# Where the two rings of split weights begin in a partition, in a float32r decoder trunk held by TensorE

## The chip, the cores and the metric

The kernel runs on one core of a Trainium2 chip. The metric is the device time of one execution in microseconds. Two timed runs of the kernel before gave 2196.1 and 2196.19 us, median 2196.14 us.

## The reference

The kernel computes a two-layer decoder trunk on 256 tokens of width 2048, all in float32:

```python
def swiglu(h, w_in, w_out):
    g, u = jnp.split(h @ w_in, 2, axis=-1)
    return (jax.nn.silu(g) * u) @ w_out
...
x = x + gla_mixer(rms_norm(x, attn_norm), gla_w_in, w_alpha2, b_alpha, head_gain, gla_w_out)
x = x + swiglu(rms_norm(x, ffn_norm[0]), ffn_w_in[0], ffn_w_out[0])
k_shared, v_shared = shared_kv(x, kv_norm, w_kv, k_norm)
x = x + diff_attention(rms_norm(x, diff_norm), k_shared, v_shared, diff_w_q, ...)
x = x + swiglu(rms_norm(x, ffn_norm[1]), ffn_w_in[1], ffn_w_out[1])
```

Here `gla_mixer` is gated linear attention in chunks of 64 tokens (4 heads), `shared_kv` one projection to normalised keys and values, and `diff_attention` attention with two softmaxes per head (8 heads). Nearly all the arithmetic is in the eight products of 256 tokens with a weight matrix: 2048 rows by 6144 columns (and 16 for the gate), 2048 by 2048, 2048 by 11264 (`w_in` of the FFN, d_ff is 5632), 5632 by 2048, then the same again with 6144 columns of keys, queries and values.

## The kernel before

**Units.** A weight matrix is worked off in blocks of 512 columns, and each block in units of 256 rows (`UNIT_KT` = 2 tiles of 128). A unit is 128 partitions by 2 x 512 float32, 4 KB in a partition. There are 784 units. SyncE's queue loads a unit into `raw`, a ring of four slots (`SLOTS`). ScalarE copies it to `w_hi` rounded to float32r, the high part (L945), and VectorE subtracts that from `raw` and writes the rest as float32r to `w_lo`, the low part (L1311). `w_hi` and `w_lo` are rings of four slots too, each 16 KB in a partition.

**Products.** The tokens are kept transposed and are split in the same way: `xT[:, 0]` is the high part, `xT[:, 1]` the low part, in tiles of 128 rows by 256 tokens. TensorE holds 128 tokens as the stationary operand (128 float32r, 512 bytes in a partition) and streams 512 columns of the weights (2048 bytes in a partition) as the moving operand. One float32 product is three float32r products, high x high, high x low and low x high, so that a unit takes 2 row tiles x 2 token halves x 3 = 12 matmuls of 128x512:

```python
def unit(src, kt, n_kt, p, slot, u):
    pe.wait_ge(lo_done, u + 1)
    for j in range(UNIT_KT):
        for tb in range(TB):
            hi = src[:, 0, kt + j, tb * P:(tb + 1) * P]
            lo = src[:, 1, kt + j, tb * P:(tb + 1) * P]
            nc.tensor.matmul(acc[p][tb][:, :], hi, w_hi[:, slot, j, :], ...)   # L639
            nc.tensor.matmul(acc[p][tb][:, :], hi, w_lo[:, slot, j, :], ...)   # L640
            last = nc.tensor.matmul(acc[p][tb][:, :], lo, w_hi[:, slot, j, :], ...)   # L641
    last.then_inc(unit_used, 1)
```

`first_unit` (L651, L656) serves the first block and `last_unit` (L667 to L669) the last unit, with the same twelve matmuls in another order. `src` is one of five stationary arrays of the same shape: `xT` (inputs of the GLA, of both FFNs and of keys and values), `g_oT`, `xT_q`, `d_oT` and `hT` (5632 rows, the hidden activations of an FFN). Every matmul is issued with a load of its stationary operand (LDWEIGHTS, engine PEld in the profile), which runs while the matmul before it streams.

**Other matmuls.** Between units stand a few hundred others. Those with plain float32 operands are shown as two instructions for each matmul: the score and value products of both attentions (L762 to L782, L882 to L900) and the transposes of `x` (L678). Those with float32r operands outside the rings are the gate: L727 multiplies `a_w` (stationary, 96 columns, 384 bytes in a partition, sixteen of them one behind the other) with the 256 tokens of `xT` (moving, always at a multiple of 512 bytes), and L740 multiplies `w_gate` (stationary, 128 columns, multiples of 512) with the 256 tokens of `a_T` (moving, at a multiple of 512).

**Order.** The order of the work is written out by hand per engine, with semaphores: TensorE waits for `lo_done` of the unit, ScalarE for the load and for the unit four back to be used, VectorE for ScalarE. The loads wait for `lo_done` of the unit four back.

**Addresses.** Arrays are laid in a partition one behind the other in the order in which `trunk` names them. A helper fills up to a wanted remainder of 512 bytes:

```python
def place(name, rest, stack=ctx):
    base = -(-nc.sbuf_base // 32) * 32
    gap = (rest - base) % 512
    if gap:
        sb(name, [P, gap // 4], F32, stack)
```

It is called with 0 ahead of `x` and ahead of `g_oT`, `hT` and the pair `xT_q`, `d_oT`. `x` (16 KB), `xT` (32 KB) and `raw` (16 KB) are whole multiples of 512, so that `w_hi` and `w_lo` begin at a multiple of 512 as well.

Of the kernel before, what the change touches and what calls it, by code (L numbers as in the profile page):

```python
# [182 lines left out]
def trunk(nc, x_in, attn_norm, gla_w_in, w_alpha2, b_alpha, gla_head_norm, gla_w_out, kv_norm, w_kv, k_norm,  # L183
          diff_norm, diff_w_q, q_norm, lq1, lk1, lq2, lk2, diff_head_norm, diff_w_out, ffn_norm, ffn_w_in,
          ffn_w_out, const_in, out):
    with ExitStack() as ctx:
        def sb(name, shape, dt=F32, stack=ctx):
            return stack.enter_context(nc.sbuf_tensor(name, shape, dt))
# [4 lines left out]
# [6 lines that stand above are left out]
# [3 lines left out]
        x = sb("x", [P, TB, D])  # L202
        xT = sb("xT", [P, 2, KT, S], F32R)
        raw = sb("raw", [P, SLOTS, UNIT_KT, CB])
        w_hi = sb("w_hi", [P, SLOTS, UNIT_KT, CB], F32R)
        w_lo = sb("w_lo", [P, SLOTS, UNIT_KT, CB], F32R)
        tok = sb("tok", [P, TB, CB])
        scratch = sb("scratch", [P, TB * CB])
        junk = sb("junk", [P, CB])
# [1541 lines left out]
```

## Time and profile before

| what | value |
|---|---|
| median of 2 timed runs | 2196.14 us (2196.1 to 2196.19) |
| profiled execution, first to last instruction (span) | 2193.8 us |
| granted TensorE clock, mean over the span | 1.000 |
| PE busy, share of the span, matmul instructions | 2188.1 us, 100%, 9720 |
| weight loads (PEld) busy | 1808.9 us, 82% |
| VectorE, ScalarE, GpSimd busy | 57%, 48%, 13% |
| bytes moved by DMA, mean rate | 447.01 MB, 204 GB/s |

A timed run is 2.3 us longer than the span of the profiled execution, the part that lies around the first and the last instruction. The matmul rows have a modelled end: a matmul of 512 columns is drawn with some 389 ns although the next begins 227 ns after it, so that a busy PE says only that the engine had work. The pace is read from the distance of the starts.

### The profile page before, as it was taken

The numbers are of one execution on the slowest core, as the hardware profiler recorded it, in microseconds if no ns is written. First come the engines' busy times: TensorE is split into PE (matmuls) and PEld (weight loads), VectorE is DVE, ScalarE is ACT, GpSimd is POOL, SyncE is SP. The second block draws the span as 40 slices with busy tenths as digits, with TensorE's granted clock in tenths as the row PEclk, the third lists the DMA queues.
The fourth block names the chain that finished last, engine by engine and source line by source line (L and its number), as shares of the span: only waits on it lengthen the run. The fifth ranks groups of instructions, "written<-read, shape, count | busy, mean of one in ns | idle before, by whom it ended". The sixth has DMA issues, their size and how long they took to land.

```text
span 2193.8 us, 27239 instructions
## 1 busy us (share of the span) xinstructions
PE 2188.1 (100%) x9720; PEld 1808.9 (82%) x9720; DVE 1242.7 (57%) x1460; ACT 1058.2 (48%) x1428; POOL 283.0 (13%) x563
## 2 busy tenths in 40 slices
PE   9999999999999999999999999999999999999999
PEld 7888788888888888888888888888888888888887
DVE  5665566655555555555566676665555555555443
ACT  6666455444444444444456665554444444444333
POOL 3210334100000000001125333341000000000000
PEclk9999999999999999999999999999999999999999
DMA  8765667666666666666667666676666666666664
GB/s 264 210 189 176 189 202 218 203 215 203 203 202 213 201 202 206 200 205 203 201 202 217 196 207 202 204 223 210 199 207 200 215 200 203 205 210 194 195 193 163
DMA packets 252675, 447.01 MB, mean 204 GB/s; under 512 B 27665, under 2 KB 41969, under 8 KB 252593
## 3 DMA queue, kind: packets, MB, share of 16 engines
q1 hardware_dynamic: 236176, 428.79, 62.2%
q0 software_dynamic: 16240, 17.07, 2.7%
q8 instruction: 49, 0.80, 0.1%
q14 instruction: 34, 0.27, 0.0%
q10 hardware_dynamic: 176, 0.07, 0.0%
HBM read 414.37 MB, written 2.10 MB: 190 GB/s over the span
## 4 chain that ended last, share of the span: by engine, by line
PE 100%; DVE 0%; ACT 0%; issue 0%; POOL 0%; DVEq 0%; ACTq 0%; POOLq 0%
PE acc L641 32%; PE acc L639 32%; PE acc L640 32%; PE acc L651 1%; PE acc L656 0%; PE side L884 0%; PE tps L678 0%; PE side L727 0%; PE side L703 0%; PE side L762 0%; PE side L882 0%; PE side L898 0%; PE side L899 0%; PE side L900 0%; PE side L782 0%; PE side L780 0%
## 5 line engine op out<-in xcount | busy, mean ns | idle before, releaser
L1311 DVE TENSOR_TENSOR w_lo<-raw,w_hi 128x1024 fp32r<-128x1024 f32 x784 | 954.8, 1222 | 835.6 <-ACT w_hi L945 831.3
L945 ACT ACTIVATE w_hi<-raw 128x1024 fp32r<-128x1024 f32 x784 | 827.8, 1059 | 1002.9 <-PE acc L641 994.0
L639 PE MATMUL acc<-w_hi,xT 128*128 128x512 f32 x2016 | 787.6, 391 | 0.0
L641 PE MATMUL acc<-w_hi,xT 128*128 128x512 f32 x2016 | 784.4, 389 | 0.0
L640 PE MATMUL acc<-w_lo,xT 128*128 128x512 f32 x2016 | 784.4, 389 | 0.0
L639 PEld LDWEIGHTS acc<-w_hi,xT 128*128 128x128 f32 x2016 | 378.4, 188 | 79.0 <-issue 0.7
L640 PEld LDWEIGHTS acc<-w_lo,xT 128*128 128x128 f32 x2016 | 378.4, 188 | 78.9 <-issue 0.7
L641 PEld LDWEIGHTS acc<-w_hi,xT 128*128 128x128 f32 x2016 | 378.4, 188 | 78.9
L639 PE MATMUL acc<-w_hi,hT 128*128 128x512 f32 x700 | 272.3, 389 | 0.0
L640 PE MATMUL acc<-w_lo,hT 128*128 128x512 f32 x700 | 272.3, 389 | 0.0
L641 PE MATMUL acc<-w_hi,hT 128*128 128x512 f32 x700 | 272.3, 389 | 0.0
L640 PEld LDWEIGHTS acc<-w_lo,hT 128*128 128x128 f32 x700 | 131.4, 188 | 27.5
L639 PEld LDWEIGHTS acc<-w_hi,hT 128*128 128x128 f32 x700 | 131.4, 188 | 27.3
L641 PEld LDWEIGHTS acc<-w_hi,hT 128*128 128x128 f32 x700 | 131.4, 188 | 27.1
L588 POOL DMA_DIRECT2D x_turned<-scratch x32 | 15.7, 500 | 580.5 <-DVE scratch L1336 580.5
L588 POOL DMA_DIRECT2D tok<-scratch x112 | 54.9, 499 | 143.2 <-DVE scratch L1336 99.5
L1560 DVE TENSOR_TENSOR hT<-tok,hT 128x512 f32 (+1 forms) x44 | 28.4, 688 | 67.1 <-ACT hT L1140 67.1
L1140 ACT ACTIVATE hT<-tok 128x512 f32 (+1 forms) x44 | 25.4, 624 | 64.1 <-DMA tok<-scratch 64.1
L639 PE MATMUL acc<-w_hi,xT_q 128*128 128x512 f32 x128 | 50.6, 396 | 0.0
L639 PE MATMUL acc<-w_hi,g_oT 128*128 128x512 f32 x128 | 50.2, 392 | 0.0
L639 PE MATMUL acc<-w_hi,d_oT 128*128 128x512 f32 x128 | 50.0, 391 | 0.0
L641 PE MATMUL acc<-w_hi,xT_q 128*128 128x512 f32 x128 | 49.9, 390 | 0.0
(204 smaller groups left out, 1372.2 us busy)
## 6 DMA issues: line engine op xcount, KB each, us to landing
raw<-in_ffn_w_in SPq DMA_DIRECT2D x352, 512.0 KB, 3.8
raw<-in_ffn_w_out SPq DMA_DIRECT2D x176, 512.0 KB, 4.7
raw<-in_gla_w_in SPq DMA_DIRECT2D x96, 512.0 KB, 4.3
raw<-in_w_kv SPq DMA_DIRECT2D x64, 512.0 KB, 4.6
raw<-in_gla_w_out SPq DMA_DIRECT2D x32, 512.0 KB, 4.9
raw<-in_diff_w_q SPq DMA_DIRECT2D x32, 512.0 KB, 4.6
raw<-in_diff_w_out SPq DMA_DIRECT2D x32, 512.0 KB, 4.9
tok<-scratch SPq DMA_DIRECT2D x352, 32.0 KB, 2.9
```

The lines of the kernel that those rows point to most:

```text
L588: pool.dma_start(dst[g * SQ:(g + 1) * SQ, s], src[s * SQ:(s + 1) * SQ, g]).then_inc(turn_moved[TURN[name, n] % 2], 16)
L639: nc.tensor.matmul(acc[p][tb][:, :], hi, w_hi[:, slot, j, :], start=(kt + j == 0), stop=False)
L640: nc.tensor.matmul(acc[p][tb][:, :], hi, w_lo[:, slot, j, :], start=False, stop=False)
L641: last = nc.tensor.matmul(acc[p][tb][:, :], lo, w_hi[:, slot, j, :], start=False, stop=(kt + j == n_kt - 1))
L651: nc.tensor.matmul(acc[p][tb][:, :], src[:, part, kt + j, tb * P:(tb + 1) * P], w_hi[:, slot, j, :], start=(kt + j == 0 and part == 0), st ...
L945: nc.scalar.activation(w_hi[:, slot, :, :], raw[:, slot, :, :], ACT.Copy).then_inc(hi_done, 1)
L1140: nc.scalar.activation(hidden(0, n, tb), turned(tb), ACT.Copy).then_inc(h_hi, 1)
L1311: nc.vector.tensor_tensor(w_lo[:, slot, :, :], raw[:, slot, :, :], w_hi[:, slot, :, :].bitcast(F32), ALU.subtract).then_inc(lo_done, 1)
L1560: nc.vector.tensor_tensor(hidden(1, n, tb), turned(tb), hidden(0, n, tb).bitcast(F32), ALU.subtract).then_inc(h_lo, 1)
```

## The change

The ring of the high parts begins 448 bytes past a multiple of 512, that of the low parts 320 bytes past one, and `tok` behind them at a multiple of 512 again. The three fillers take 448, 384 and 192 bytes in a partition, 1024 together, so that all arrays behind the rings (`tok` and `scratch` up to the stationary arrays `g_oT`, `hT`, `xT_q` and `d_oT`) move up by 1024 bytes and keep their remainders. `x`, `xT` and `raw` stay where they were. No instruction is added, removed or moved on any engine; only the addresses in the operands differ.

```diff
         raw = sb("raw", [P, SLOTS, UNIT_KT, CB])
+        place("gap_hi", 448)
         w_hi = sb("w_hi", [P, SLOTS, UNIT_KT, CB], F32R)
+        place("gap_lo", 320)
         w_lo = sb("w_lo", [P, SLOTS, UNIT_KT, CB], F32R)
+        place("gap_tok", 0)
         tok = sb("tok", [P, TB, CB])
```

## Rows read from the trace of the kernel before

**Rows 1.** Page, parts 1 and 2: busy time; granted clock and DMA in 40 slices.

```profile
PE 2188.1 (100%) x9720; PEld 1808.9 (82%) x9720; DVE 1242.7 (57%) x1460; ACT 1058.2 (48%) x1428; POOL 283.0 (13%) x563
...
PEclk9999999999999999999999999999999999999999
DMA  8765667666666666666667666676666666666664
```

**Rows 2.** Page, part 4: the chain that ended last, by line.

```profile
PE acc L641 32%; PE acc L639 32%; PE acc L640 32%; PE acc L651 1%; PE acc L656 0%; PE side L884 0%; PE tps L678 0%; PE side L727 0%; PE side L703 0%; PE side L762 0%; PE side L882 0%; PE side L898 0%; PE side L899 0%; PE side L900 0%; PE side L782 0%; PE side L780 0%
```

**Rows 3.** Page, part 5: out<-in xcount | busy, mean ns | idle before, releaser.

```profile
L1311 DVE TENSOR_TENSOR w_lo<-raw,w_hi 128x1024 fp32r<-128x1024 f32 x784 | 954.8, 1222 | 835.6 <-ACT w_hi L945 831.3
L945 ACT ACTIVATE w_hi<-raw 128x1024 fp32r<-128x1024 f32 x784 | 827.8, 1059 | 1002.9 <-PE acc L641 994.0
L639 PE MATMUL acc<-w_hi,xT 128*128 128x512 f32 x2016 | 787.6, 391 | 0.0
...
L639 PE MATMUL acc<-w_hi,hT 128*128 128x512 f32 x700 | 272.3, 389 | 0.0
```

**Rows 4.** Windows: stretch, length, busy (x) of PE, PEld, DVE, ACT, POOL; clock, DMA.

```profile
500.00:1100.00 600.00, 600.00 (x2649) 496.82 (x2648) 317.34 (x311) 260.35 (x279) 23.54 (x48) 1.00 0.64 204
...
1240.00:1390.00 150.00, 150.00 (x681) 125.10 (x680) 108.92 (x180) 90.56 (x207) 55.43 (x109) 1.00 0.65 200
```

**Rows 5.** Chain in order of time, diff attention's value products: start, us, what.

```profile
1341.88 0.43 PE side L898 x2
1342.32 0.43 PE side L899 x2
1342.75 0.43 PE side L900 x2
1343.18 0.43 PE side L898 x2
1343.61 0.43 PE side L899 x2
1344.04 0.43 PE side L900 x2
1344.47 0.23 PE acc L639
```

**Rows 6.** One line each: matmul duration in ns, min/median/max, then starts.

```profile
L640 PE MATMUL acc<-w_lo,xT x2016: 387/389/398, 32.8 to 1950.3; 128*128 128x512 f32 x184
L898 PE MATMUL side<-d_v,d_at x16: 377/379/409, 1328.2 to 1386.6; 128*128 128x256 f32 x16
L740 PE MATMUL side<-a_T,w_gate x8: 282/283/283, 53.2 to 59.5; 96*128 96x256 f32 x8
L882 PE MATMUL side<-d_k,d_q x32: 270/273/275, 1241.2 to 1322.2; 128*128 128x128 f32 x32
L727 PE MATMUL side<-xT,a_w x32: 274/280/284, 38.0 to 41.7; 128*96 128x256 f32 x32
```

**Rows 7.** Timeline of PE behind the scores of a head: start, us, instruction.

```profile
1242.28 0.58 PE L639 MATMUL acc<-w_hi,xT_q 128*128 128x512 f32 x1
1242.69 0.40 PE L640 MATMUL acc<-w_lo,xT_q 128*128 128x512 f32 x1
1242.93 0.40 PE L641 MATMUL acc<-w_hi,xT_q 128*128 128x512 f32 x1
...
1243.62 0.39 PE L641 MATMUL acc<-w_hi,xT_q 128*128 128x512 f32 x1
...
1244.55 0.39 PE L639 MATMUL acc<-w_hi,xT_q 128*128 128x512 f32 x1
1244.78 0.39 PE L640 MATMUL acc<-w_lo,xT_q 128*128 128x512 f32 x1
```

**Rows 8.** Chain in order of time, the gate's products.

```profile
38.21 3.77 PE side L727 x32
...
53.34 0.48 PE side L740 x4
```

**Rows 9.** VectorE's and ScalarE's splits: duration in ns, min/median/max, starts.

```profile
L1311 DVE TENSOR_TENSOR w_lo<-raw,w_hi x780: 1179/1225/1239, 20.7 to 2180.6; 128x1024 fp32r<-128x1024 f32 x195
...
L945 ACT ACTIVATE w_hi<-raw x780: 1037/1061/1095, 19.6 to 2179.5; 128x1024 fp32r<-128x1024 f32 x195
```

## The prediction, made before the changed kernel was run

> **What bounds the kernel now.** I read the page's busy line and clock first, then the chain of waits, then the groups of instructions, then the windows by stage. The busy line says PE 100% and the clock row shows a 9 in all 40 slices [rows 1]; the granted clock is 1.00 in the windows [rows 4], so the level is 2.4 GHz and there is nothing to win or lose there. The chain that ended last is PE alone, 96% of it in L639, L640 and L641 [rows 2]. The matmul groups have no idle time ahead of them, while VectorE and ScalarE idle for 835.6 and 1002.9 us, ScalarE for PE's release of a slot and VectorE for ScalarE [rows 3]. So nothing feeds TensorE too late. What sets the time is how many matmuls there are and how far apart they start.
>
> Their number: 784 units of 12, so 9408 matmuls of 128x512. Their pace: from 500 to 1100 us, where nothing but units runs, 2649 matmuls lie in 600 us [rows 4], 226.5 ns each, or 226.7 when the one that reaches in from ahead is not counted. 9408 x 226.7 is 2133 us of the 2193.8. The other 61 us are the start, the other matmuls and their hand-overs, and the end; the change does not reach them.
>
> Is 226.7 ns the engine's own pace for 512 columns? 512 columns at 2.4 GHz take 213.3 ns. The value products of the diff attention give a row to hold against it: plain float32, twelve instructions in 2.59 us (1341.88 to 1344.47) [rows 5], 215.8 ns each. They are 256 columns each, and at two array cycles a column (my reading of the pace: 215.8 ns are 518 cycles) that is the same 512 cycles, with stationary loads of 128 columns beside them as in the units. They have 2.5 ns over the array's own time, the units 13.4. So each unit matmul carries **10.9 ns** that this row does not have. The modelled durations say the same from another side: 379 ns for L898, 389 for L640 [rows 6]. The plain float32 product reads its moving operand at half the bytes per cycle, the float32r one at the full 4 bytes per cycle, while the next stationary operand is read. A clash of these two reads fits the difference; that it is a clash, and that it depends on addresses, is what the change stands or falls by.
>
> **What the trace says about addresses.** In the kernel before every stationary slice and every moving slice of a unit begins at a multiple of 512 bytes. So does L740, float32r with 256 columns: four in 0.48 us, 120 ns each [rows 8], against 109 for 256 cycles plus the 2.5; again about 11 too many. L727 is the one place where relative addresses vary: its stationary slices step by 384 bytes, its moving ones stay at multiples of 512. It takes 3.77 us for 32 [rows 8], 117.8 ns each, and its durations spread from 274 to 284 around 280, where the aligned L740 is at 282 to 283 throughout and the unhindered float32 L882, also 256 cycles, at 273 [rows 6]. So at other relative positions the excess goes down to about 1 ns (274 against 273), and also up to 11. Two things weaken the row. Its loads are of 96 columns and not 128, and scaled by that its mean excess (117.8 - 109.2 = 8.6, times 128/96) is 11.5 ns: on average over its positions nothing is won. And it steps in multiples of 128 bytes, while 448 and 320 are odd multiples of 64; no row shows such a position.
>
> The excess also depends on timing. Behind the scores of a head the same unit matmuls with the same remainders run unevenly: from 1242.69 to 1244.78 us nine starts take 2.09 us [rows 7], 232.2 ns each, with single steps between 0.22 (1243.40 to 1243.62) and 0.24, before they fall into the even 226.7. L640's durations run from 387 to 398 for one and the same form [rows 6]. A price that moves with the relative timing of two streams is a clash of accesses, not a fixed cost of the instruction. That is my main reason to expect that the addresses matter.
>
> **The change, part by part.** (1) Moving operand `w_hi`, 448 bytes past a multiple of 512: two of three matmuls in a unit, 6272 of 9408. (2) Moving operand `w_lo`, 320 bytes past: 3136 of 9408. Bounds for each from the rows above: the whole excess goes, -10.9 ns (L898's pace); nothing changes, 0; or the streams no longer settle and run at the uneven pace throughout, +5.5 ns (232.2 - 226.7). For all 9408: -102 us, 0, +52 us. I take the value nearest to the best positions that L727 shows: its least duration leaves 1 ns, and since that is one position of 96 columns I allow 2 to 3 ns for a whole load of 128, an estimate from 274 against 273 and the 128/96. With 2.2 ns left, the step is 218.0 ns and the sum is 9408 x -8.7 = **-82 us**.
>
> (3) ScalarE writes `w_hi` and VectorE reads `raw` (unmoved) and `w_hi` and writes `w_lo` at new remainders. Their instructions last 1037 to 1095 and 1179 to 1239 ns now [rows 9], and the spread, 4 to 5%, is a bound for what positions do to them either way. Both are hidden: a unit lasts 2.72 us on TensorE (2.62 at 218.0 ns), ScalarE needs 1.06 of it and VectorE 1.22, in the densest stretch VectorE is busy 108.9 of 150 us [rows 4], which becomes 76% when the stretch shrinks by 4%. The four slots are the cover. If both durations grew by 5% the pair would take 2.4 us one after the other, and they work on different units, so the cost stays nothing. (4) The loads land in `raw`, unmoved; the DMA engines are at 0.64 busy and 204 GB/s [rows 4], and 4% more rate brings 0.67. Nothing. (5) Everything behind the rings moves by 1024 bytes and keeps its remainder of 512; the L727, L740 and float32 products should keep their times. Between nothing and the 11 ns of excess for the 40 float32r ones, under 0.5 us either way.
>
> Sum against the profiled execution: 2193.8 - 82 = 2112; with the 2.3 us around it, **2114 us**, 3.7% under the median of 2196.14.
>
> **Rivals.** (a) *The excess has nothing to do with addresses.* It could be a fixed price of a 128-column float32r load beside a full-rate stream: L740 and the settled units both pay 11 ns, and L727's mean pays the same per column loaded. Against it stands the spread of one form in L727 and L640. Time: 2196, no change. The Trainium skill speaks for this rival, and against the change: "TensorE: Matmul & The Clock Gate", Part 2, first step, gives TensorE two independent read ports and says that loading the next weights takes no read bandwidth from the running matmul. By that rule alone neither the 10.9 ns nor a gain from new positions would exist, and this case's trace already disagrees on the first, 226.7 against 215.8 ns.
>
> (b) *Only one of the two rings lies well.* The best position may be one thing and the other neutral. If only `w_lo` gains 8.7 ns: 3136 x 8.7 = 27 us, 2169. If only `w_hi`: 55 us, 2142. Also here: both keep half of the excess, 51 us, 2145.
>
> (c) *Slower: the streams never settle.* Now each step of a unit has the same relation of its two reads, and it settles on an even pace within about ten matmuls. After the change the three products of a row tile have two relations in turn (448 and 320 past), so that each hand-over from `w_hi` to `w_lo` and back shifts the moving read against the load and the pace may stay the uneven one. Price 5.5 ns for each, 9408 times: 2196 + 52 = 2248. It decides wherever the step of a settled unit is above 226.7 ns. For it speaks that L727, whose relation changes from one matmul to the next, varies all along; against it, that the variation there goes mostly below the aligned 283.
>
> (d) *The excess goes entirely:* 2196 - 102 = 2094, the floor of this change.
>
> **How the numbers follow.** Forecast and (d), excess mostly or wholly gone, 2090 to 2130: 0.44. (b) 0.17, of which two thirds (0.12) lie under 2152, where 2% begins. (a) 0.24. (c) 0.15. Two per cent, 44 us, is about what a measurement of this kernel is taken to tell from no change. Faster by more: 0.44 + 0.12 = 0.56; within: 0.05 + 0.24 = 0.29; slower by more: 0.15. The range reaches from just under the floor, 2090, over all of (d), (b) and (a) to 2200, and leaves out (c) alone.
>
> **What would show it.** In the profile after, the window from 500 us on gives the step: more than 2700 matmuls in 600 us if the forecast holds (218 ns is 2752, the floor 2780), 2649 for (a), about 2584 for (c). The duration of L640 should fall from 389 towards 379, and L639 and L641 with it; if only one falls, it is (b). L898, L740 and L727 should stay. PE should still have no idle ahead of it, with VectorE's and ScalarE's waits for PE shorter by what PE gains. I am wrong if the step stays at 226.7 (the clash is blind to positions), if it grows, or if VectorE's split becomes so slow that PE waits for `lo_done`.

## The result, and the profile after

The changed kernel takes 2236.97 us (2236.96 to 2236.99, two runs) against 2196.14: ratio 1.0186, 95% interval 1.0156 to 1.0215. It is 41 us slower, clear of the noise, though the interval leaves open whether by more than 2%; the forecast was 82 us faster.

Page of the kernel after, parts 1, 2 and 4 (busy time, granted clock, chain by line):

```profile
PE 2229.6 (100%) x9720; PEld 1810.3 (81%) x9720; DVE 1242.5 (56%) x1460; ACT 1058.1 (47%) x1428; POOL 281.0 (13%) x563
...
PEclk9999999999999999999999999999999999999999
...
PE acc L644 32%; PE acc L642 32%; PE acc L643 32%; PE acc L654 1%; PE acc L659 0%; PE side L887 0%; PE tps L681 0%; PE side L706 0%; PE side L730 0%; PE side L765 0%; PE side L885 0%; PE side L901 0%; PE side L902 0%; PE side L903 0%; PE side L785 0%; PE side L784 0%
```

All lines stand three further down (L639 is L642 now). The picture is that of [rows 1, 2]: the same 9720 matmuls, full clock, TensorE alone on the chain. Nobody else became late. Part 5 of the same page (count | busy, mean ns | idle before, releaser):

```profile
L1314 DVE TENSOR_TENSOR w_lo<-raw,w_hi 128x1024 fp32r<-128x1024 f32 x784 | 954.4, 1222 | 870.0 <-ACT w_hi L948 865.6
L948 ACT ACTIVATE w_hi<-raw 128x1024 fp32r<-128x1024 f32 x784 | 827.9, 1059 | 1039.3 <-PE acc L644 1032.2
L644 PE MATMUL acc<-w_hi,xT 128*128 128x512 f32 x2016 | 796.0, 395 | 0.0
L642 PE MATMUL acc<-w_hi,xT 128*128 128x512 f32 x2016 | 795.5, 395 | 0.0
L643 PE MATMUL acc<-w_lo,xT 128*128 128x512 f32 x2016 | 787.8, 391 | 0.0
```

The two splits cost what they did [rows 3], to the nanosecond, although both touch moved rings; their idle time grew by 34 and 36 us, since TensorE releases slots later. The matmuls are drawn with 395, 391 and 395 ns where [rows 3] has 391 and 389. The pace, in the window of units alone:

```profile
500.00:1100.00 600.00, 600.00 (x2598) 487.46 (x2597) 314.19 (x309) 257.09 (x278) 23.54 (x48) 1.00 0.67 200
```

2598 matmuls in place of the 2649 of [rows 4]; from the first start in the window to the last, 231.1 ns each in place of 226.7. Spread over the kernel: (2235.2 - 2193.8) / 9408 = 4.4 ns for each unit matmul, and that is the whole result. Durations by line (min/median/max) of three of the lines of [rows 6]:

```profile
L643 PE MATMUL acc<-w_lo,xT x2016: 388/391/399, 33.7 to 1987.0; 128*128 128x512 f32 x184
L743 PE MATMUL side<-a_T,w_gate x8: 278/283/288, 54.3 to 60.7; 96*128 96x256 f32 x8
L730 PE MATMUL side<-xT,a_w x32: 274/280/284, 39.0 to 42.6; 128*96 128x256 f32 x32
```

What was not moved against its partner keeps its median: 283 ns for L743, 280 for L730, and also 379 for L901 (L898 before) and 273 for L885 (L882). L743's spread grew from 282 to 283 ns to 278 to 288, though both its operands kept their remainders: other matmuls run around it now. And the timeline of PE in the middle of an FFN, where nothing but units has run for 200 us:

```profile
700.27 0.40 PE L642 MATMUL acc<-w_hi,xT 128*128 128x512 f32 x1
700.51 0.39 PE L643 MATMUL acc<-w_lo,xT 128*128 128x512 f32 x1
700.74 0.39 PE L644 MATMUL acc<-w_hi,xT 128*128 128x512 f32 x1
700.97 0.39 PE L642 MATMUL acc<-w_hi,xT 128*128 128x512 f32 x1
701.19 0.39 PE L643 MATMUL acc<-w_lo,xT 128*128 128x512 f32 x1
701.42 0.39 PE L644 MATMUL acc<-w_hi,xT 128*128 128x512 f32 x1
701.66 0.39 PE L642 MATMUL acc<-w_hi,xT 128*128 128x512 f32 x1
701.89 0.39 PE L643 MATMUL acc<-w_lo,xT 128*128 128x512 f32 x1
702.12 0.40 PE L644 MATMUL acc<-w_hi,xT 128*128 128x512 f32 x1
```

The steps go 0.24, 0.23, 0.23, 0.22, 0.23, 0.24, 0.23, 0.23: the unevenness that [rows 7] shows for some ten matmuls behind a break now never ends. In whole nanoseconds the starts show a cycle of nine steps that comes again and again, 236, 235, 231, 230, 226, 230, 233, 233, 226, with a mean of 231.1.

### The profile page after: what moved, and what is told of

Same layout as the page of the kernel before. It is cut to its first block, busy times and chain, and to the rows that moved or that the text cites. A ratio compares the mean times of both kernels' runs of the same rounds, so it can differ in the third digit from the quotient of the medians.

```text
span 2235.2 us, 27239 instructions
## 1 busy us (share of the span) xinstructions
PE 2229.6 (100%) x9720; PEld 1810.3 (81%) x9720; DVE 1242.5 (56%) x1460; ACT 1058.1 (47%) x1428; POOL 281.0 (13%) x563
## 4 chain that ended last, share of the span: by engine, by line
PE 100%; DVE 0%; ACT 0%; issue 0%; POOL 0%; DVEq 0%; ACTq 0%; POOLq 0%
PE acc L644 32%; PE acc L642 32%; PE acc L643 32%; PE acc L654 1%; PE acc L659 0%; PE side L887 0%; PE tps L681 0%; PE side L706 0%; PE side L730 0%; PE side L765 0%; PE side L885 0%; PE side L901 0%; PE side L902 0%; PE side L903 0%; PE side L785 0%; PE side L784 0%
## 5 line engine op out<-in xcount | busy, mean ns | idle before, releaser
L1314 DVE TENSOR_TENSOR w_lo<-raw,w_hi 128x1024 fp32r<-128x1024 f32 x784 | 954.4, 1222 | 870.0 <-ACT w_hi L948 865.6
L948 ACT ACTIVATE w_hi<-raw 128x1024 fp32r<-128x1024 f32 x784 | 827.9, 1059 | 1039.3 <-PE acc L644 1032.2
L644 PE MATMUL acc<-w_hi,xT 128*128 128x512 f32 x2016 | 796.0, 395 | 0.0
L642 PE MATMUL acc<-w_hi,xT 128*128 128x512 f32 x2016 | 795.5, 395 | 0.0
L642 PEld LDWEIGHTS acc<-w_hi,xT 128*128 128x128 f32 x2016 | 378.5, 188 | 84.5 <-issue 0.7
L644 PE MATMUL acc<-w_hi,hT 128*128 128x512 f32 x700 | 276.4, 395 | 0.0
L642 PE MATMUL acc<-w_hi,hT 128*128 128x512 f32 x700 | 275.1, 393 | 0.0
L642 PEld LDWEIGHTS acc<-w_hi,hT 128*128 128x128 f32 x700 | 131.4, 188 | 29.3
L591 POOL DMA_DIRECT2D tok<-scratch x112 | 54.9, 499 | 146.7 <-DVE scratch L1339 101.9
L642 PE MATMUL acc<-w_hi,xT_q 128*128 128x512 f32 x128 | 51.1, 399 | 0.0
L642 PE MATMUL acc<-w_hi,g_oT 128*128 128x512 f32 x128 | 50.7, 396 | 0.0
L644 PE MATMUL acc<-w_hi,g_oT 128*128 128x512 f32 x128 | 50.6, 395 | 0.0
```

The lines of the kernel that those rows point to most:

```text
L591: pool.dma_start(dst[g * SQ:(g + 1) * SQ, s], src[s * SQ:(s + 1) * SQ, g]).then_inc(turn_moved[TURN[name, n] % 2], 16)
L948: nc.scalar.activation(w_hi[:, slot, :, :], raw[:, slot, :, :], ACT.Copy).then_inc(hi_done, 1)
L1314: nc.vector.tensor_tensor(w_lo[:, slot, :, :], raw[:, slot, :, :], w_hi[:, slot, :, :].bitcast(F32), ALU.subtract).then_inc(lo_done, 1)
```

## The experiments

### One ring at a time, and both alike

The obvious theories after the result: two different relations in turn keep the pace from settling (rival (c)), or each remainder has its own price. `e1` keeps only the high ring's move, `e2` only the low ring's, `e3` gives both the same. (The two lines that each run changes stand here on one line.)

```diff
-        place("gap_hi", 448)    place("gap_lo", 320)    # the change
+        place("gap_hi", 448)    place("gap_lo", 0)      # e1
+        place("gap_hi", 0)      place("gap_lo", 320)    # e2
+        place("gap_hi", 448)    place("gap_lo", 448)    # e3
```

e1: 

> Only the high ring is moved (448), the low ring begins at a multiple of 512. Alternation: 2230 to 2245 us, the same as after the change, since the two rings still differ. Position: the high ring's part alone, 6272 matmuls at +5.6 ns (L642 and L644 after the change are at 231.7 and 232.8 ns from start to start), 2231 us, with L643 back at 226.7 ns.

e2: 

> Only the low ring is moved (320). Alternation: 2225 to 2245 us. Position: the low ring's part alone, 3136 matmuls at +2.2 ns (L643 after the change is at 228.9 ns), 2203 us.

e3: 

> Both rings at 448, so that all twelve matmuls of a unit have one relation to the stationary slices. Alternation: the pace settles as before, 226.7 ns, 2196 us. Position: all 9408 pay the high ring's +5.6 ns, 2249 us.

Measured against 2195.85 us of the kernel before in the same job: e1 2267.96 us (1.0328, 1.0308 to 1.0349), e2 2244.88 us (1.0223, 1.0203 to 1.0244), e3 2257.59 us (1.0281, 1.0264 to 1.0298). The window from 500 to 1100 us of e1 and e3, one row from each; e2 has 2588 matmuls in it:

```profile
500.00:1100.00 600.00, 600.00 (x2561) 480.46 (x2560) 307.93 (x298) 252.10 (x272) 23.61 (x48) 1.00 0.66 198
```

```profile
500.00:1100.00 600.00, 600.00 (x2573) 483.45 (x2572) 309.51 (x301) 255.79 (x277) 23.54 (x48) 1.00 0.66 198
```

Both theories fall. One relation for all twelve matmuls (e3) is not 2196 but 62 us slower than before, so alternation is not the cause, or at least not the only one. And the prices do not add: the high ring alone costs 72 us and the low ring alone 49, where both moves together cost 41 and I had expected 35 and 7 for the parts. The page of e1 shows the matmuls of the ring that was not moved among the dearest:

```profile
L643 PE MATMUL acc<-w_lo,xT 128*128 128x512 f32 x2016 | 803.6, 399 | 0.0
```

The pace belongs to the pair, not to a ring.

### A map of the pace

`m1` measures the disputed cost by itself: TensorE issues the three products of a unit, 48 matmuls for each pair of remainders, with no other engine at work. It computes nothing of the trunk. Like `m2` to `m4` below it was run once; the windows read of it have a granted clock of 1.00.

```python
...
for i in range(8):
    for j in range(8):
        segment(xT, hi[i], lo[j], acc)     # rings at 64 i and 64 j; order as in unit
for i in range(8):
    segment(xs, hi[i], lo[i], acc)         # stationary array at 64
...
```

> A kernel of its own: TensorE alone, float32r matmuls of 128x512 with stationary slices at multiples of 512 in the order of a unit (high x high, high x low, low x high), 48 in a row for each of the 64 pairs of remainders (64 i for the high ring, 64 j for the low ring); it computes nothing of the trunk and returns x. Then the stationary arrays 64 past a multiple of 512 with both rings at the same remainder, then stationary slices of 64 columns in place of 128, then one slice pair repeated. If the pace depends on remainders, pair (0, 0) settles at 226.7 ns a matmul and pair (448, 320) lies at 231 as in the kernel. Theory 'alternation' (two relations in turn keep the streams from settling): the pairs with i = j all settle at 226.7 and most others lie above. Theory 'position' (each remainder has its own price): the time of a pair is a sum of a price of i and a price of j, and i = j = 448 is dearer than (448, 320). If the excess is a clash with the weight load, 64 columns halve it (pace 220 to 222 at (0, 0)); if it is a fixed price it stays at 226.7.

Mean ns from start to start over the last 36 steps of each 48, worked out from the starts in the trace (rows: high ring at 0, 64, 128 and 192; columns: low ring at the same; the other three quarters of the map have 256 added to one or both). Most pairs never become even but run in a cycle of 2 to 15 steps or more, so that an entry moves by up to 0.4 ns with the steps that are averaged:

```
          lo 0    64     128    192
hi   0   226.7  232.2  233.3  228.9
hi  64   231.1  228.9  231.1  230.4
hi 128   228.8  228.9  232.4  231.2
hi 192   234.4  231.1  231.1  233.3

stationary array at 64, both rings at 0, 64, 128, 192:  233.3  226.7  228.9  232.4
```

The other three quarters repeat the rows of 0, 128 and 192 within 0.12 ns. The row of 64 repeats when 256 is added to the high ring, and with 256 added to the low one it has 233.3, 228.9, 232.2 and 230.4. Whether that is owed to the address or to the 48 matmuls that ran before is not shown: (64, 0) runs behind (0, 448), (64, 256) behind (64, 192). So, but for that row, the remainder of 256 counts, and the kernel before sat on the **lowest value of the map**. The change's pair, (448, 320), is (192, 64) modulo 256: 231.1 in its four entries. The last row repeats the map's diagonal (226.7, 228.9, 232.4, 233.3) shifted by one: what counts on this grid is the distance of the moving from the stationary operand. Neither "alternation" nor "position" as a sum describes the table.

The map gives the whole kernels' times: 2195.9 + 9408 x (pace - 226.67), with the unrounded paces.

```
              pair (hi, lo) mod 256      map, ns   by the map   measured, us
the change    192, 64                    231.1     2238         2236.97
e1            192, 0                     234.4     2269         2267.96
e2            0, 64                      232.2     2247         2244.88
e3            192, 192                   233.3     2259         2257.59
e4            0, 0    (hi ring at 256)   226.7     2196         2196.22
e5            0, 0    (all at 64)        226.7     2196         2196.18
e6            -64     (stationary at 64) 233.3     2259         2257.09
e7            192, 64                    231.1     2238         2236.98
```

For the change and e1 to e3 this was worked out after their times were known; for e4 to e7 what the distance gives (2196, 2196, 2259 and 2237) was written down before they ran. The map also meets the pace inside the kernels: from 500 to 1100 us the starts of the change, e1, e2 and e3 lie 231.1, 234.4, 232.0 and 233.3 ns apart, and the change's steps go through the same cycle of nine as pair (448, 320) does in `m1`. `m1` has no splits and hardly any DMA traffic (a share of 0.01) beside TensorE, so neither is needed for the slower pace.

`m1` also ran 64 stationary columns. With both rings at 0 they take 230.0 ns, neither the 220 to 222 of a clash with the weight load nor the 226.7 of a fixed price; at (448, 320) they take 229.6.

e4 to e7 test it on the kernel itself: a ring moved by 256; rings and all five stationary arrays moved by 64 together; the stationary arrays alone; and the change's remainders less 256. In e5 and e6 `raw` and the arrays behind `hT` and `d_oT` come to lie 64 further as well; no unit matmul reads them.

e4: 

> The whole kernel with the high ring at 256 and the low ring at 0. If only the distance between moving and stationary operand modulo 256 counts, as the map says (pair 256, 0 at 226.7 ns), it takes 2196 us. If any two different remainders of 512 disturb the pace, or any distance from a multiple of 512, it is above 2230 us.

e5: 

> The whole kernel with both rings and all five stationary arrays at 64 past a multiple of 512. If only the distance between moving and stationary operand counts, 2196 us. If a multiple of 256 is what matters by itself, the pace is that of the first map's pair (64, 64), 228.8 ns, and the time 2216 us.

e6: 

> The whole kernel with both rings at a multiple of 512, as before, and the five stationary arrays at 64 past one. If the distance alone counts, the pace is that of distance -64, 233.3 ns in the first map, and the time 2196 + 9408 x 6.7 = 2259 us. If only the rings' own position counts, 2196 us.

e7: 

> The whole kernel with the high ring at 192 and the low ring at 64: the change's remainders less 256 each. If positions count modulo 256, it is the changed kernel again, 2237 us. If they count modulo 512, another pace.

```diff
+        place("gap_xT", 64)
         xT = sb("xT", [P, 2, KT, S], F32R)
-            place("gap_g", 0, s1)      # and gap_h, gap_d
+            place("gap_g", 64, s1)     # e5, and e6 with both rings at 0
```

Ratios to the kernel before in the same job: e4 0.9999 (0.9988 to 1.0011), e5 1.0000 (0.9989 to 1.0012), e6 1.0279 (1.0258 to 1.0299), e7 1.0188 (1.0171 to 1.0205). The same window from e6; e4 and e5 have 2649 matmuls in it, e7 has 2598:

```profile
500.00:1100.00 600.00, 600.00 (x2573) 480.86 (x2572) 309.39 (x301) 255.05 (x277) 23.55 (x48) 1.00 0.67 198
```

2649 is the kernel before, 2598 is the changed kernel, and e6 with its distance of -64 has the 2573 of e3, whose distance is 192, the same modulo 256. In e6 neither ring that TensorE reads was moved at all. Its steps are 233 or 234 ns throughout, as even as the 226 and 227 of the kernel before and 6.7 ns longer; in e3 they alternate between 231 and 235 or 236, with the same mean.

### Is there anything below 226.7, and what is the excess?

`m2` and `m4` look for a better remainder in steps of 16 and 8 bytes; `m2` and `m3` take the excess apart.

m2: 

> TensorE alone again; nothing of the trunk is computed and x is returned. Both rings at the same remainder r, in steps of 16 bytes from 0 to 240, 48 matmuls each; then one slice pair repeated, with the moving slice at r in steps of 8 bytes, 24 each; then stationary slices of 32, 64, 96 and 128 columns and moving slices of 256 to 512 columns at r = 0; last bf16 on both sides. The first map gave 226.6, 229.2, 231.7 and 233.4 ns for one slice pair at 0, 64, 128 and 192, and 0 again at 256. Theory 'sawtooth': the pace rises with r up to a break between 192 and 256 and is below 226.6 just above the break, so that some remainder beats the kernel before. Theory 'zero is the floor': nothing lies under 226.6. If the excess is a number of clashes with the weight load, 32 columns come down to about 218.5 (2.5 + a quarter of 10.9 over 213.3); if it is a wait for a slot it stays at 226.7 for every width, and falls in steps with the moving columns. bf16 should lie at 215.8.

m3: 

> TensorE alone; nothing of the trunk is computed and x is returned. (1) Moving slices of 400 to 512 columns in steps of 8: a clash spread over the stream makes the step grow evenly with the columns; a hand-over that waits for a slot makes it a staircase of 6.7 ns (256, 320, 384 and 512 columns lay 13.3 ns over their array time, 448 columns 20.0). (2) A float32r matmul and a bf16 matmul in turn: if the price is paid by the float32r stream while a 4-byte stationary operand is read beside it, neither step has more than 2.5 ns, since each load now runs beside the other kind; if it belongs to the start or end of a float32r stream, one of the two steps keeps about 13 ns. (3) A float32r matmul and a plain float32 matmul in turn. (4) The stationary slice in steps of 16 bytes, with 32 columns and with 128: if only the distance of the two starting addresses counts, the 32-column row repeats the 128-column row; if the reading matters, the two differ.

m4: 

> TensorE alone; nothing of the trunk is computed and x is returned. All 256 pairs of remainders of the high and the low ring in steps of 16 bytes, 36 matmuls each in a unit's order. Theory 'zero is the floor': no pair lies under 226.6 ns, and the pairs at 226.7 are few. Rival: some pair of two different remainders settles lower, at 220.0 or 215.8 ns, and would make the kernel 63 to 102 us faster.

Worked out from the starts in the traces of m2 and m3, mean ns from start to start once the pace has settled or goes in its cycle (the columns row gives the excess over columns / 2.4):

```
both rings at 0 16 32 48:        226.7 231.7 233.3 233.3
           at 64 80 96 112:      228.9 231.1 233.3 231.1
           at 128 144 160 176:   232.4 233.3 234.4 233.3
           at 192 208 224 240:   233.3 234.6 233.3 226.7
stationary columns 32 64 96 128: 231.7 230.0 230.0 226.7   (m2, all slices at 0)
moving columns 256 320 384 448 512, excess:  13.3 13.3 13.3 20.0 13.3   (m2)
moving columns 400 424 448 472 488 512, excess:  13.3 16.7 15.8 16.7 22.4 13.3   (m3)
bf16, 512 columns:               215.9
```

In m4 the 256 pairs average 231.8 ns, the dearest takes 242.2, and four lie at 226.7: (0, 0), (48, 224), (112, 240) and (192, 16). None is lower. "Sawtooth" and the hope for 220.0 or 215.8 ns are gone; zero is the floor of what was tried, and no version came out that beats the kernel before. The sweeps of one repeated slice pair agree: with the moving slice moved in steps of 8 bytes (m2) the least is 226.6 at 0, with the stationary one in steps of 16 (m3) 226.6 to 226.7 at 0, 16 and 240.

The excess is not what I took it for. With a quarter of the stationary columns the load reads a quarter of the bytes, and the pace is 231.7 instead of the 218.5 that a clash spread over the load would leave; in m3, with the stationary slice at sixteen positions, 32 columns take 229.1 to 239.9 ns, at some positions more than 128 columns and at others less. So how much is loaded plays a part, but it is not a saving in proportion. Where the pace is even, the excess is 13.3 ns for 256 columns as for 512, so it does not grow along the stream. Between 400 and 512 columns it goes up and down between 13.3 and 22.4 ns, which is neither the even growth nor the staircase of 6.7 ns that m3 was built to tell apart. And it does not need a 4-byte load beside a 4-byte stream. The timeline of m3, float32r (the `hi` rows) and bf16 (the `narrow` rows) in turn, where each load runs beside the other kind:

```profile
107.85 0.58 PE L89 MATMUL one<-hi,xT 128*128 128x512 f32 x1
108.27 0.39 PE L89 MATMUL one<-narrow,narrow_s 128*128 128x512 bf16 x1
108.31 0.58 PE L89 MATMUL one<-hi,xT 128*128 128x512 f32 x1
```

A pair takes 0.46 us (107.85 to 108.31), 33 ns over the 427 of its 1024 columns, where bf16 alone pays 2.5 ns for each matmul (m2, steps of 215 and 216 ns) and float32r alone 13.3. Here a load and the stream beside it are never both of 4 bytes, and the pair still pays 17 ns more than the two do alone. With plain float32 in place of bf16 (m3 too) the pair takes 1087 ns against 1085 for the two alone, so nothing is added. The excess comes with the float32r matmul and its neighbours, not only with two 4-byte float32r reads at once. Where the excess is 13.3 or 20.0 ns the steps are multiples of 6.67 ns (120.0, 146.7, 173.3, 180.0, 206.7, 226.7), as if a float32r stream had to begin on a beat. These widths are all multiples of 16 columns, which are 6.67 ns themselves, so this says no more than that the excess is two or three times 6.67; and one steady row of m2 (moving slice at 104 bytes) runs at 230.0, which is none. The beat is a reading that no run tested.

## Why the prediction was wrong

**What bounds the kernel**: right. TensorE alone, 9408 matmuls at one pace, everybody else hidden. The time moved by exactly the change of that pace.

**That the addresses decide the pace**: right, and rival (a), no influence, fell: the same instructions take 2196 or 2268 us by where the rings lie.

**The step that failed** is the value of parts (1) and (2), -8.7 ns for each of 9408 matmuls, taken from L727's least duration; measured, it is +4.4 ns. It had two errors. First, I read the 10.9 ns over the float32 row as a clash of two reads that another position would relieve. The map, m2 and m4 show that in none of some 300 relations tried did a settled or mean pace fall below 226.6; the 10.9 (13.3 with the 2.5) is a price that every float32r matmul of this shape paid at the least, wherever its operands lay. Second, I took L727's minimum as the nearest row. It is the duration of one matmul in an uneven sequence of another form (96 stationary and 256 moving columns): from start to start L727 takes 112 to 121 ns, the 112 between 119 and 117 and 2 to 3 ns over L882's 109 to 110, where the durations said 1, as the map's cycles have single steps of 224 and 225 beside others of 241. L727's mean was no safe row either. It is 117.8 ns, 2.2 under the aligned L740; the prediction turned this into 11.5 ns, nothing won, only by scaling with 128/96, and the runs don't bear that scaling out: at distance 0, 32, 64 and 96 stationary columns take more time than 128. Unscaled it would have said 21 us faster, the wrong sign again. The row that counted was the one of the same form, [rows 7]: the kernel's own matmuls take 226 or 227 ns where they are settled, through nearly the whole FFN, and 232.2 where they are not. That is the value of +5.5 ns which the prediction had among its bounds and gave to rival (c).

**Rival (c), slower**: it had the sign, the place and nearly the size: the uneven pace of [rows 7] throughout, +5.5 ns foretold, +4.4 measured, 2248 against 2237. Its cause was wrong. It blamed the turn between two relations, and e3, with one relation, is slower still, as is e6, whose pace is even; in the map and m2 only a distance of 0 modulo 256 (or 240, m2) settles at 226.7 when both rings are alike. What it gave as its point of decision, a step above 226.7, was right but said nothing about when.

**Parts (3) to (5)**: right. (The spreads of [rows 9] are 5 to 6%, not 4 to 5; nothing hangs on it.) The splits take 1222 and 1059 ns as before although they read and write moved rings, the loads are unchanged, and L730, L885 and L901 keep their medians. That later arrays moved by 1024 bytes cost nothing that shows. Rival (b), only one of the two rings lies well, had the wrong picture: e1 and e2, each moving one ring, are both slower than moving both.

The Trainium skill's rule that I weighed, "TensorE: Matmul & The Clock Gate", Part 2, first step, that loading the next weights takes no read bandwidth from the running matmul, fits the columns: at distance 0, 32 stationary columns are no cheaper than 128 (231.7 against 226.7 ns in m2). Taken as a reason that positions can't matter, as rival (a) took it, it does not hold here: e6 moved the stationary arrays and neither ring, and each step took 6.5 ns more.

**Open**: why the float32r step has its excess, and what the distance does to it. The distance of the remainders is a rule found, not a mechanism. The pace also depends on what ran before, or on something else that these runs did not hold fixed: 448 moving columns at distance 0 ran at 206.7 ns in m2 and at 202.5 in m3, behind different neighbours and into another PSUM tile, and the pair (128, 128) at 232.4 in m1 and 233.5 in m4. In steps of 16 bytes the distance alone does not fix the pace either: the moving slice at 240 ran at 226.7 in a unit's order and at 236.8 as one repeated pair, both in m2, and the same distance made by moving the stationary slice to 16 gives 226.6 for a repeated pair (m3). L727 says so too: its distances modulo 256 take only two values, since a stationary step is 384 bytes, but its steps repeat only after sixteen matmuls.

## What to carry to other kernels

A gap over the ideal is no proof that it can be closed. Ask first what rows of the same form show where something varied, on average and not at their best, and do not scale a row of another form to yours by a ratio that no row tests. An even pace is no proof either way: the kernel before and e6 are both even, at 226.7 and 233.3 ns. Where only addresses differ, a kernel of TensorE alone maps all candidates in one run; its map gives eight whole kernels within 3 us of 2200, four of them before they ran. For float32r matmuls with full 512-column streams, keep moving and stationary operands at the same remainder of 256 bytes.

## What the runs showed of the hardware that was not expected

- The pace of float32r matmuls of 128x512 depends on the distance between the starting addresses of moving and stationary operand, on a 64-byte grid with period 256 in all but one row: 226.7 ns where both rings are at a multiple of 256, 228.8 to 234.4 ns at the other pairs (m1, e1 to e7), up to 242.2 ns on a 16-byte grid (m4).
- With 128 stationary columns the least excess over columns / 2.4 GHz is 13.3 ns a matmul, for 256, 320, 384, 400 and 512 moving columns (m2, m3); bf16 pays 2.5. L727, with 96 stationary and 256 moving columns, pays 11.1 on average, by steps of 112 to 121 ns.
- With fewer stationary columns at distance 0 the pace gets worse: 231.7, 230.0 and 230.0 ns for 32, 64 and 96 against 226.7 for 128 (m2).
- A float32r and a bf16 matmul in turn take 230 ns each, more than either alone (m3); a float32r and a plain float32 matmul in turn take within 2 ns of what they take alone.
